# Layer one's attention: half of the pieces of three modulation vectors summed by GpSimd instead of VectorE

## What is computed

```python
c_act = jax.nn.silu(c)
for layer in range(DEPTH):
    mod = c_act @ ada_w[layer] + ada_b[layer]
    shift1, scale1, gate1, shift2, scale2, gate2 = jnp.split(mod, 6, axis=-1)
    h = modulate(rmsnorm(x, norm1_w[layer]), shift1, scale1)
    ...                                   # layer 0: pooling and chunk_attention, 8 heads
    x = x + gate1[:, None, :] * mix
    h2 = modulate(rmsnorm(x, norm2_w[layer]), shift2, scale2)
    ...                                   # mixture of experts
```

## Time and profile before

| | |
|---|---|
| times of three runs | 2819.82, 2821.59 and 2824.32 us, median 2821.59 us |
| the profiled execution | 2821.0 us, of which its span is 2819.3 us |
| TensorE matmul busy | 2553.6 us, 91% of the span |
| VectorE busy | 1790.0 us, 63% |
| GpSimd busy | 1462.8 us, 52% |
| attention of layer one, first head to the start of mixout | 201.7 to 279.9 us |
| TensorE's granted clock over the span | 0.932 of full |

### The profile page before, as it was taken

The page is one execution under the profiler, slowest core; times in us unless marked ns, Lnnn a source line. Parts: engine busy times, 40 slices in busy tenths (PEclk is TensorE's granted clock), DMA queues, the critical chain, the costliest instruction groups (busy, mean ns, idle before and its releaser), DMA issues.

```text
span 2819.3 us, 36780 instructions
## 1 busy us (share of the span) xinstructions
PE 2553.6 (91%) x12750; PEld 2002.6 (71%) x12750; DVE 1790.0 (63%) x2191; ACT 963.6 (34%) x1494; POOL 1462.8 (52%) x1234
## 2 busy tenths in 40 slices
PE   4978989969999998999498989999995889999998
PEld 3754777847777777788386358888884768888887
DVE  6769866757777776667688556666135954666324
ACT  2013267723443432677312323222013632222102
POOL 4730334435544553344465016666777837666775
PEclk8977889979999998999799689999997999999999
DMA  8745479942233223798432113333231123333222
GB/s 311 255 144 204 176 260 329 325 152 84 81 99 96 85 80 107 279 342 300 134 79 79 56 45 96 99 93 98 97 116 45 38 53 90 104 89 104 88 92 82
DMA packets 319122, 386.73 MB, mean 137 GB/s; under 512 B 51578, under 2 KB 259214, under 8 KB 318902
## 3 DMA queue, kind: packets, MB, share of 16 engines
q1 hardware_dynamic: 261424, 335.84, 36.3%
q10 hardware_dynamic: 34438, 28.08, 3.3%
q0 software_dynamic: 23168, 21.59, 2.3%
HBM read 397.62 MB, written 55.41 MB: 161 GB/s over the span
## 4 chain that ended last, share of the span: by engine, by line
PE 36%; POOL 20%; issue 19%; DVE 13%; DMA 9%; ACT 2%; SPq 0%; ACTq 0%; POOLq 0%; DVEq 0%
POOL WL L836 14%; PE PAIR L528 6%; PE PAIR L529 5%; PE PAIR L530 5%; POOL WH L832 5%; PE PAIR L1840 4%; PE BANK L528 2%; PE BANK L529 2%; PE BANK L530 2%; PE PAIR L1810 2%; PE BANK L2279 2%; DMA RAW<-in_ffn_w_up 2%; DMA RAW<-in_moe_w 2%; DVE ADA_SUM L633 1%; DVE ADA_SUM L631 1%
## 5 line engine op out<-in xcount | busy, mean ns | idle before, releaser
L836 POOL TENSOR_TENSOR WL<-RAW,WH 128x512 fp32r<-128x512 f32 x584 | 819.2, 1432 | 12.2
L528 PE MATMUL PAIR<-HH,WH 128*128 128x512 f32 x1792 | 712.4, 398 | 50.4 <-POOL HL L1125 28.8
L529 PE MATMUL PAIR<-HL,WH 128*128 128x512 f32 x1792 | 703.1, 392 | 0.0
L530 PE MATMUL PAIR<-HH,WL 128*128 128x512 f32 x1792 | 701.9, 392 | 0.0
L831 POOL TENSOR_TENSOR TURN<-ONES 128x1 f32<-128x1 f32 x146 | 33.7, 231 | 932.0 <-PE PAIR L530 854.5
L528 PEld LDWEIGHTS PAIR<-HH,WH 128*128 128x128 f32 x1792 | 339.6, 190 | 134.1 <-issue 46.1
L530 PEld LDWEIGHTS PAIR<-HH,WL 128*128 128x128 f32 x1792 | 339.7, 190 | 72.1
L529 PEld LDWEIGHTS PAIR<-HL,WH 128*128 128x128 f32 x1792 | 339.9, 190 | 71.4 <-issue 2.4
L832 POOL TENSOR_SCALAR WH<-RAW 128x2048 fp32r<-128x2048 f32 x146 | 282.3, 1934 | 0.0
L2014 POOL DMA_INDIRECT XG<-htok_scratch,GATHER_I x78 | 106.2, 1362 | 259.2 <-PE PAIR L1810 147.7
L528 PE MATMUL BANK<-WH,GH 128*128 128x256 f32 x624 | 180.7, 290 | 0.0
(11 more groups left out here) (525 smaller groups left out, 4883.8 us busy)
## 6 DMA issues: line engine op xcount, KB each, us to landing
RAW<-in_moe_w SPq DMA_DIRECT2D x156, 512.0 KB, 7.0
RAW<-in_ffn_w_up SPq DMA_DIRECT2D x88, 512.0 KB, 4.6
W2RAW<-in_moe_w SPq DMA_DIRECT2D x78, 512.0 KB, 5.9
ADA_B<-in_ada_w SPq DMA_DIRECT2D x30, 1024.0 KB, 5.5
RAW<-in_ssm_w_in SPq DMA_DIRECT2D x48, 512.0 KB, 4.8
ADA_A<-in_ada_w SPq DMA_DIRECT2D x18, 1024.0 KB, 7.8
RAW<-in_ffn_w_down SPq DMA_DIRECT2D x32, 512.0 KB, 3.9
RAW<-in_ev_w_in SPq DMA_DIRECT2D x20, 512.0 KB, 4.8
```

What stands on the lines that cost most here:

```text
L528: nc.tensor.matmul(o, wh, xh, start=start, stop=False)
L529: nc.tensor.matmul(o, wh, xl, start=False, stop=False)
L530: return nc.tensor.matmul(o, wl, xh, start=False, stop=stop)
L836: ins = pool.tensor_tensor(WL[:, s, c], RAW[:, s, c], WH[:, s, c].bitcast(F32), ALU.subtract)
```

## The change

For the three vectors q = 6, 7 and 8 (pieces 24 to 35) the pieces with j = 2 and 3 go to GpSimd. They are the pieces 26, 27, 30, 31, 34 and 35, which VectorE summed in heads 1, 3 and 5. GpSimd has no instruction in the kernel that multiplies and adds at once, so it multiplies each half of a piece in place and adds it to a sum of its own, `ADA_SUM3`; a first product goes straight into that sum. TensorE then sums both 128x1024 sums for each vector: 16 matmuls in place of eight, in accumulating pairs. A new semaphore, `ada_pool_used`, counts GpSimd's pieces. TensorE waits for it in `pe_ada`, SyncE's queue waits for it before it loads into a place that GpSimd's piece had, and GpSimd waits for `ada_added` before it overwrites the sum of the vector before. `pool_ada` stands in GpSimd's program after the split of mixout's second unit.

```diff
+    def ada_pooled(n):
+        return 24 <= n < 36 and n % 4 >= 2
+
+    def ada_counts(n):
+        pooled = sum(ada_pooled(i) for i in range(n))
+        return n - pooled, pooled
+
+    def pool_ada(pool):
+        for n in [n for n in range(24, 36) if ada_pooled(n)]:
+            q, j = n // 4, n % 4
+            slot, uses, _ = ada_place(n)
+            pool.e.wait_ge(ada_landed[slot], 16 * (uses + 1))
+            if j == 2:
+                if q > 6:
+                    pool.e.wait_ge(ada_added, q - 6)
+            for m in range(2):
+                piece = ada_piece(slot)[:, m, :]
+                first = j == 2 and m == 0
+                pool.link(pool.e.tensor_scalar(ADA_SUM3[:] if first else piece, piece, C_ACT[:, 2 * j + m:2 * j + m + 1], None, ALU.mult))
+                if not first:
+                    ins = pool.e.tensor_tensor(ADA_SUM3[:], ADA_SUM3[:], piece, ALU.add)
+                    if m == 0:
+                        pool.link(ins)
+            ins.then_inc(ada_pool_used, 1)
+            pool.e.wait_ge(ada_pool_used, ada_counts(n + 1)[1])
+
     def dve_ada(dve, first, last):
-        for n in range(first, last):
+        for n in [n for n in range(first, last) if not ada_pooled(n)]:
...
-                dve.e.wait_ge(ada_used, n)
+                dve.e.wait_ge(ada_used, ada_counts(n)[0])
...
     def pe_ada(pe, q, o=None):
-        pe.e.wait_ge(ada_used, 4 * (q + 1))
+        pe.e.wait_ge(ada_used, ada_counts(4 * (q + 1))[0])
+        if 6 <= q < 9:
+            pe.e.wait_ge(ada_pool_used, ada_counts(4 * (q + 1))[1])
...
-            ins = nc.tensor.matmul(o[:, m:m + 1], ada_sum(q)[:, m * P:m * P + P], ONES[:, 0:1], start=True, stop=True)
+            sums = (ada_sum(q), ADA_SUM3) if 6 <= q < 9 else (ada_sum(q),)
+            for i, part in enumerate(sums):
+                ins = nc.tensor.matmul(o[:, m:m + 1], part[:, m * P:m * P + P], ONES[:, 0:1], start=i == 0, stop=i == len(sums) - 1)
...
-                    sp.wait_ge(ada_used, before + 1)
+                    if ada_pooled(before):
+                        sp.wait_ge(ada_pool_used, ada_counts(before + 1)[1])
+                    else:
+                        sp.wait_ge(ada_used, ada_counts(before + 1)[0])
...
-        split_units(pool.e, 6, plan.u["moe0"])
+        split_units(pool.e, 6, plan.u["mixout"] + 2)
+        pool_ada(pool)
+        split_units(pool.e, plan.u["mixout"] + 2, plan.u["moe0"])
```

More of the change, by code:

```diff
@@ L499, in build @@
     ada_landed = [sem(f"ada_landed{i}") for i in range(4)]
-    ada_used, ada_added = sem("ada_used"), sem("ada_added")
+    ada_used, ada_added, ada_pool_used = sem("ada_used"), sem("ada_added"), sem("ada_pool_used")
     c_ready = sem("c_ready")
```

## The result

The changed kernel takes 2867.56 us (median of four runs, 2864.43 to 2868.86) against 2822.11 us before: a ratio of 1.0161, with a 95% interval of 1.0148 to 1.0174. That is 45.5 us slower. The forecast was 22.9 us slower, with a range up to 36.5. The sign and the chain of waits were right; one term of the sum, the price of GpSimd's multiplication, was far too small, and the loss came out at half of its size.

The account below looks back on a forecast made before the run. TensorE was taken to bound even heads, VectorE odd ones, leaving 2.15 us a pair to gain. Against VectorE's -15.4 us, GpSimd's loop put 22.9 us on the path: 2844.5 us, range 2830.5 to 2858.

Parts of the forecast that it names:

- What bounds the stage: Attention head pairs: TensorE limits even heads, VectorE odd ones; lighter VectorE can give only 2.15 us of idle TensorE per pair.
- the 15.4 of the rival: Rival: VectorE is the bound and all its 15.4 us are gained, 2806.2 us; shares the chance of "GpSimd is in time".
- The loop: Head pair: matmuls 7.1, waiting 0.1, transposes 2.3, scores 4.6, to L656's end 2.5, GpSimd 13.0: 29.6 us, not 21.7.
- handed on in full behind head 6: From `turned(6)` to mixout: still 14.4 us, so the 22.9 us delay reaches mixout whole, starting at 302.9.
- The price of the multiplication: GpSimd's 128x1024 multiplication: 1.0 us, from half of a 128x2048 row of 1.89 us with a fixed part.
- a doubling: Column factor on GpSimd's multiplications: if it doubles them, 4 us a vector, 12 us by itself, 34.9 us late, 2856.5 us.
- The additions: GpSimd's 128x1024 addition: 2.5 us undisturbed, 3.9 us beside VectorE's `ada`.
- The disturbance: GpSimd slowed beside VectorE's normalisation and one own piece: 1.0 us added a vector, 12.0 becoming 13.0 us.
- The loads: SyncE's loads in the loop don't end later: piece 31 lands at T6 + 13.4, GpSimd starting piece 30 at T6 + 16.6.
- The clock stays up for the 32 matmuls: Rival, matmuls before heads 2, 4, 6: 3.9 us in place of 7.1, 13.3 us late, 2834.9 us; chance 0.20.
- GpSimd is slower than the nearest rows: Rival, GpSimd's sums: every addition disturbed, 32.8 us late, 2854.4 us, or dearer column factors, 2856.5; chance 0.12.
- GpSimd is in time: Rival: both pieces summed within 8.2 us, TensorE never waits; 2821.0 us, or 2811.4 if the clock stays up; chance 0.08.

Follow-up runs that it names:

- left_out_16: Kernel before with pieces 26, 27, 30, 31, 34 and 35 neither loaded nor summed, 16 matmuls a vector: ratio 0.9983 (-4.8 us).
- left_out_32: As left_out_16, but with the change's 32 matmuls a vector, reading VectorE's sum twice: ratio 1.0008 (+2.3 us over the kernel before).
- one_sum: Changed kernel with TensorE summing only VectorE's part, 16 matmuls in place of 32, every wait kept: 2859.4 us, ratio 1.0121.
- const_factor: Changed kernel with GpSimd's multiplications taking two constants of 1.0 instead of a column: 2846.9 us, ratio 1.0078.
- price: Kernel before with GpSimd, in an idle stretch, running several multiplication forms and an addition three times on an unused tile: ratio 1.0032 (+9.0 us).
- two_op_after_norm: two_op, with GpSimd starting the sums of q = 7 and 8 only after VectorE's normalisation of heads 3 and 5: ratio 1.0077 (+21.7 us).
- two_op: Changed kernel with a second operation, times 1.0, behind the column in each GpSimd multiplication, same result: 2847.33 us, ratio 1.0095.
- no_gate: Changed kernel without TensorE's wait for GpSimd and its sum, or GpSimd's wait for the vector before; loads' waits stay: ratio 1.0090 (+25.4 us).
- one_piece: Changed kernel with GpSimd taking only the pieces with j = 3 (27, 31, 35), VectorE keeping the others: ratio 1.0032 (+9.0 us).
- two_op_one_piece: one_piece with the edits of two_op and two_op_after_norm: ratio 1.0007 (+2.0 us over the kernel before).

## Why the prediction was wrong

**What bounds the stage: right.** The reading of the earlier trace rows, that VectorE's 97% in the odd heads is worth its 2.15 us of TensorE's idle time and no more, gave 6.5 us for the whole of VectorE's relief. left_out_16 measured 4.8 (0.6 to 9.3), far from the 15.4 of the rival. That it is near 6.5 is in part luck: the clock, the new idle stretch and a shorter way behind head 6 (12.3 us in place of 14.4) aren't in that sum and moved it both ways. And 16 more matmuls leave nothing of it (left_out_32).

**The loop: right for the change as it was built.** The 32 matmuls at half clock (7.1 forecast, 6.96 measured, and one_sum), transposes and scores, L690 as what releases GpSimd, then GpSimd, then TensorE again. The delay of mixout adds up by the forecast's own steps. GpSimd's three sums are 6.5, 6.7 and 6.7 us longer, and the first piece landed 1.3 us later (210.44 for 209.1). That is 21.2 us on top of 22.9, 44.1 in all, and 43.9 was measured. It was handed on in full behind head 6, as forecast. With the cheap multiplications that the forecast assumed, though, the loop isn't the forecast's: in const_factor TensorE never waits for GpSimd.

**The price of the multiplication: wrong, and it is the step that failed.** "A 128x2048 multiplication takes 1.89 us, so half of it with a fixed part is 1.0 us" took its price from a row of another form. L832 multiplies by two constants; the change multiplies once. I took one operation to be no dearer than two. It takes 2.84 to 3.16 us. Twelve of them are 24 us longer than forecast. The additions were a little cheaper, and the 1.0 us a vector that was added for disturbance is already inside the measured operations; that leaves the 19.9 us by which the three sums are longer. The forecast saw the other difference, the column, and bounded it by a doubling. That bound had no row behind it, and the form of the instruction hadn't been asked about at all. With 2.84 us from the run price in place of 1.0, and all else as forecast, a vector takes 7.4 us more, and the sum gives 22.9 + 22.1 = 45.0 us and 2866.6; measured were 45.5 and 2867.56.

**The additions: right.** 2.5 us forecast, 2.34 to 2.36 measured, and 2.65 once. The Trainium skill's figure in "GPSIMD Engine Reference", section "Performance versus the Vector engine", gives an estimate of 2.25 us, and the trace agrees within 0.1 us. Its selection table in section "When to use GPSIMD" calls operations with one input "roughly line-rate" on GpSimd; the trace shows that only for the form with two operations, 1.04 us for 1024.

**The disturbance: half of it was left out.** I added 1.0 us to GpSimd and nothing to VectorE's path. In the second vector GpSimd's four multiplications took 12.1 us, where four undisturbed ones of the run price make 11.4, so GpSimd lost about 0.8 us. VectorE lost up to 1.7 us in one normalisation of the change (3.00 for 1.27), and up to 5.1 us beside the faster multiplications (6.34 in two_op_after_norm). In the change most of it is hidden behind the wait for GpSimd; in const_factor and two_op it is part of what is late next. That these two landed near the 2844.5 us of the forecast is chance: their pairs take 28.1 to 30.1 us where my sum has 29.6, but the last term is TensorE and the normalisation, where I had GpSimd.

**The loads: right for the change.** I wrote that piece 31 lands ahead of the time when GpSimd wants it, and neither the second nor the third vector waited for a load there. It has less to spare than I thought. no_gate shows the loads as a lock of their own, of 27 to 28 us a pair with GpSimd's slow multiplications and not the 24.7 that I expected of that run, since a load that could go waits in SyncE's queue behind one that can't. In one_piece one vector did wait for its load.

**The rivals.** "The clock stays up for the 32 matmuls" fell for the change. In left_out_32, where TensorE doesn't wait before them, it held for two of the three vectors (3.73 us at a granted clock of 1.00); the other took 4.91 us at 0.74. So my argument against it, that 32 such matmuls let the clock fall by themselves, isn't borne out. "GpSimd is slower than the nearest rows" was the one that came true, beyond its own price and by the form, not the column. "GpSimd is in time" fell for the change; left_out_32, where TensorE never waits for GpSimd, and two_op_one_piece, where it waits once, show no gain from it.

## What to carry to other kernels

An operation that the trace doesn't show has to be priced in its own form, with the number of its operations, its kind of factor and its inputs; if that form has no row, the upper end of the range is several times the nearest one, or it is measured first, as the run price did in a stretch where GpSimd idles (such a stretch isn't free: the kernel took 9.0 us longer). When a share of a busy engine's work is handed to another, read first who waits for that engine: here its 97% were worth about 2 us a pair, and the new helper stood in front of TensorE, which was the bound. A queue in order turns a late reader of one buffer into a late load of all that stand behind it.

## What the runs showed of the hardware

- GpSimd's multiplication of 128x1024 by one factor takes 2.78 us with a constant and 2.84 with a column; with a second factor of 1.0 behind it, 1.04 with constants and 1.12 with the column. These are undisturbed. Why the single form is slower wasn't found.
- VectorE's multiplications by a column with source and target in SBUF are slowed by GpSimd. The four of a normalisation take 1.27 us alone, 1.8 to 4.2 where they met the single-factor multiplications and their additions, and 4.2 to 6.3 beside the two-factor ones and theirs. The row maxima (1.67 us) don't change, and the operations that read PSUM hardly do (1.68 us for four, 1.76 once in price).
- VectorE's multiply-and-add of 128x1024, with two inputs from SBUF, takes 1.28 us alone and up to 3.24 beside GpSimd (the change), and slows GpSimd in turn: 1.98 for 1.12 us in two_op_one_piece, 3.92 for 2.84 in price. The Trainium skill, "GPSIMD Engine Reference", section "Key points", says that GpSimd shares memory interfaces with VectorE and that the contention is with VectorE's two-port modes and with two inputs from SBUF. The rows agree on the second. No row names a mode; the multiplications, which are hit hardest, are the form that runs faster alone (0.75 us for 128x1024 against 1.28). The rows add how much: up to five times (6.34 for 1.27 us).
- The granted clock of TensorE was 0.50 for the 32 one-column matmuls where TensorE had stood waiting for GpSimd longest, in the change (4.8 and 11.6 us), in one_piece (3.4 and 2.5 us) and in two_op_after_norm (6.5 us): they took 6.96 us. After 1.2 and 1.8 us of waiting (two_op_one_piece, two_op_after_norm) they took 5.23 and 5.13 us, at 0.68 and 0.70. Where TensorE hadn't waited they took 3.73 to 4.91 us, at 1.00 to 0.74 (left_out_32, const_factor, two_op), and 3.70 us after 0.45 us of waiting (one_piece). Not waiting isn't enough: in price 16 of them took 3.58 us at 0.50 behind a head that had run at half clock.
